# Slot numbers of all experts spread over the units of the second chunk of expert 0

## What is computed

```python
def moe_swiglu(h, w_router, w_gu_e, w_down_e):
    probs = jax.nn.softmax((hf @ w_router).astype(F32), axis=-1)
    topv, topi = lax.top_k(probs, TOP_K)                 # 2 of 8 experts
    topv = topv / jnp.sum(topv, axis=-1, keepdims=True)
    gates = jnp.sum(jax.nn.one_hot(topi, N_EXPERTS, dtype=F32) * topv[..., None], axis=1)
    for e in range(N_EXPERTS):
        out = out + gates[:, e:e + 1] * swiglu(hf, w_gu_e[e], w_down_e[e]).astype(F32)
```

## Time and profile before

| what | value |
|---|---|
| three runs | 1415.29, 1418.67, 1419.31 us |
| median | 1418.67 us |
| the profiled execution, own time | 1415.88 us |
| its span | 1414.1 us |
| mean granted TensorE clock | 0.984 of full speed |
| PE busy | 1355.0 us (96%) |
| DVE busy | 1116.7 us (79%) |
| ACT busy | 810.1 us (57%) |
| POOL busy | 242.8 us (17%) |
| DMA | 409.75 MB, mean 290 GB/s |
| chain that ended last | PE 88%, POOL 4%, DVE 3%, DMA 2% |

### The profile page before, as it was taken

How to read it: one execution, slowest core, us unless ns; L and a number is a source line. 1 busy time by engine, 2 the same in 40 slices (tenths; PEclk the granted TensorE clock), 3 DMA queues, 4 the chain that set the end, 5 groups by cost and what they waited for, 6 DMA issues and landing times.

```text
span 1414.1 us, 17000 instructions
## 1 busy us (share of the span) xinstructions
PE 1355.0 (96%) x6717; PEld 1128.6 (80%) x6717; DVE 1116.7 (79%) x1024; ACT 810.1 (57%) x808; POOL 242.8 (17%) x347
## 2 busy tenths in 40 slices
PE   4999979899999998989999999999999999999995
PEld 2787558699999986888888888888888888888884
DVE  2697766557677556658899899998998999989997
ACT  4432764523223223355687777777777777767772
POOL 4000681100000014001899300000000000000001
PEclk9999989999999999989999999999999999999998
DMA  9967445945554537537899999999999999999991
GB/s 311 366 227 248 133 144 183 333 154 178 172 169 147 190 132 248 214 135 283 267 403 390 370 412 369 375 398 347 414 373 370 412 353 388 392 355 401 373 413 51
DMA packets 119238, 409.75 MB, mean 290 GB/s; under 512 B 8385, under 2 KB 31090, under 8 KB 102258
## 3 DMA queue, kind: packets, MB, share of 16 engines
q1 hardware_dynamic: 111376, 382.24, 72.1%
q0 software_dynamic: 6704, 23.14, 5.3%
q10 hardware_dynamic: 1074, 3.23, 0.6%
HBM read 398.58 MB, written 9.99 MB: 289 GB/s over the span
## 4 chain that ended last, share of the span: by engine, by line
PE 88%; POOL 4%; DVE 3%; DMA 2%; SPq 1%; issue 1%; ACT 1%; POOLq 0%; DVEq 0%; ACTq 0%
PE ps L1763 27%; PE ps L1765 26%; PE ps L1764 26%; DMA raw<-in_ada_w 2%; PE ps L2136 1%; POOL xn L719 1%; POOL o_rstd L717 1%; SPq L501 1%; DVE ring_lo L1561 1%; PE ps L2036 1%; POOL o_msq L715 1%; PE ps L1981 1%; POOL o_eps L712 1%; PE ps L2079 1%; PE ps L2109 1%
## 5 line engine op out<-in xcount | busy, mean ns | idle before, releaser
L1561 DVE TENSOR_TENSOR ring_lo<-raw,ring_hi 128x2048 fp32r<-128x2048 f32 (+1 forms) x210 | 451.8, 2168 | 49.6 <-ACT ring_hi L1023 49.0
L1023 ACT ACTIVATE ring_hi<-raw 128x2048 fp32r<-128x2048 f32 (+1 forms) x210 | 381.2, 1819 | 124.3 <-PE ps L1765 123.2
L1763 PE MATMUL ps<-ring_hi,xe 128*128 128x512 f32 x536 | 212.2, 396 | 1.3 <-DVE xe L1612 0.8
L1765 PE MATMUL ps<-ring_lo,xe 128*128 128x512 f32 x536 | 209.9, 392 | 0.0
L1764 PE MATMUL ps<-ring_hi,xe 128*128 128x512 f32 x536 | 209.5, 391 | 0.0
L818 ACT ACTIVATE ring_hi<-raw 128x2048 fp32r<-128x2048 f32 x53 | 101.2, 1914 | 160.9 <-PE ps L1765 149.2
L1167 DVE TENSOR_TENSOR ring_lo<-raw,ring_hi 128x2048 fp32r<-128x2048 f32 x53 | 120.4, 2288 | 87.4 <-ACT ring_hi L818 87.2
L1561 DVE TENSOR_TENSOR ring_lo_more<-raw,ring_hi_more 128x2048 fp32r<-128x2048 f32 (+1 forms) x70 | 151.8, 2168 | 16.7 <-ACT ring_hi_more L1023 16.5
L1023 ACT ACTIVATE ring_hi_more<-raw 128x2048 fp32r<-128x2048 f32 (+1 forms) x70 | 127.3, 1819 | 40.1 <-PE ps L1765 39.8
L1763 PEld LDWEIGHTS ps<-ring_hi,xe 128*128 128x128 f32 x536 | 101.5, 189 | 22.1 <-DVE xe L1612 0.9
L1765 PEld LDWEIGHTS ps<-ring_lo,xe 128*128 128x128 f32 x536 | 101.2, 189 | 21.6
(11 more groups left out here) (319 smaller groups left out, 2432.4 us busy)
## 6 DMA issues: line engine op xcount, KB each, us to landing
raw<-in_w_gu_e SPq DMA_DIRECT2D x128, 1024.0 KB, 8.1
raw<-in_w_down_e SPq DMA_DIRECT2D x88, 1024.0 KB, 8.9
raw<-in_w_gu_e SPq DMA_DIRECT2D x64, 768.0 KB, 6.8
raw<-in_ada_w SPq DMA_DIRECT2D x40, 1024.0 KB, 6.0
raw<-in_w_gu SPq DMA_DIRECT2D x44, 512.0 KB, 5.0
raw<-in_w_qkv SPq DMA_DIRECT2D x12, 1024.0 KB, 10.1
raw<-in_w_down SPq DMA_DIRECT2D x11, 1024.0 KB, 5.2
raw<-in_ada_w SPq DMA_DIRECT2D x16, 512.0 KB, 12.7
```

Of the source, the lines that this page charges most:

```text
L1023: act.activation(ehi[m % RINGM][:, 0:w], raw[:, (MOE_U0 + m) % RAW, 0:w], ACT.Copy).then_inc(hi_ready, 1)
L1561: dve.tensor_tensor(elo[m % RINGM][:, 0:w], raw[:, (MOE_U0 + m) % RAW, 0:w], ehi[m % RINGM][:, 0:w].bitcast(F32), ALU.subtract).then_inc(l ...
L1763: pe.matmul(out, l_hi, r_hi, start=first, stop=False)
L1765: return pe.matmul(out, l_hi, r_lo, start=False, stop=last)
```

## The change

`number_others()` in front of unit 8 is gone. In its place `number_some(n)` runs before unit n of the second chunk of expert 0: experts 4, 5 and 6 before n = 1, experts 0, 1 and 2 before n = 3, experts 3 and 7 before n = 4, and the transposes of `selx` before n = 5. The numbers go to bank 4 and the transposes to bank 5, which the down products use first from unit 16 on. VectorE's `numbers_out` and ScalarE's copy of `selT` move from the end of the first chunk to the turn of n = 6 (unit 14). TensorE waits for both in front of unit 16 and no longer at `TURN_K`.

```diff
+NUMBERS_AT = {1: (4, 5, 6), 3: (0, 1, 2), 4: (3, 7)}
+NUMBERS_K = 5
...
                     if kind == "gu" and n == KC - 1:
                         tanh_gate(e, c)
-                        if (e, c) == (0, 0):
-                            act.wait_ge(selT_ps, 1)
-                            act.activation(selT[:], ps[:, 7, 0:TOK], ACT.Copy).then_inc(selT_sb, 1)
...
                 kind, e, c, n = MU[m]
+                if (kind, e, c, n) == ("gu", 0, 1, NUMBERS_K + 1):
+                    act.wait_ge(selT_ps, 1)
+                    act.activation(selT[:], ps[:, 5, 0:TOK], ACT.Copy).then_inc(selT_sb, 1)
...
-            numbers_of = ps[:, 6, 64:80].rearrange("p (e c) -> p e c", c=2)
+            numbers_of = ps[:, 4, 64:80].rearrange("p (e c) -> p e c", c=2)
...
                         hidden(e, c)
-                        if (e, c) == (0, 0):
-                            numbers_out()
...
                 kind, e, c, n = MU[m]
+                if (kind, e, c, n) == ("gu", 0, 1, NUMBERS_K + 1):
+                    numbers_out()
...
-            def number_others():
-                pe.wait_ge(cnt_ready, 1)
-                for e in range(N_EXP):
+            def number_some(n):
+
+                for e in NUMBERS_AT.get(n, ()):
                     number_slots(e)
-                for k in range(TILES):
-                    ins = pe.transpose(ps[:, 7, k * P:(k + 1) * P], selx[:, k, :], ident[:])
-                ins.then_inc(selT_ps, 1)
+                if n == NUMBERS_K:
+                    for k in range(TILES):
+                        ins = pe.transpose(ps[:, 5, k * P:(k + 1) * P], selx[:, k, :], ident[:])
+                    ins.then_inc(selT_ps, 1)
...
-                    if n == 0 and (e, c) == (0, 1):
-                        number_others()
+                    if (e, c) == (0, 1):
+                        number_some(n)
                     if n == 0 and NC * e + c:
                         pe.wait_ge(eh_ready, NC * e + c)
                     if n == TURN_K and (e, c) == (0, 1):
-                        pe.wait_ge(selT_sb, 1)
-                        pe.wait_ge(idx_ready, 1)
+                        pe.wait_ge(cnt_ready, 1)
...
                         if c == 0 and e:
                             pe.wait_ge(y_sb, e)
+                        elif c == 0:
+                            pe.wait_ge(selT_sb, 1)
+                            pe.wait_ge(idx_ready, 1)
```

More of the change, by code:

```diff
@@ L2116, in number_slots @@
                 for k in range(TILES):
-                    ins = pe.matmul(ps[:, 6, 64 + 2 * e:66 + 2 * e], choice[e][:, k, :], vals[:, k, e, :],
+                    ins = pe.matmul(ps[:, 4, 64 + 2 * e:66 + 2 * e], choice[e][:, k, :], vals[:, k, e, :],
                                     start=(k == 0), stop=(k == TILES - 1))
```

## The result

The changed kernel takes 1433.63 us (median of 4 runs, 1431.08 to 1436.75) against 1418.42 for the kernel before on the same chip. The ratio is 1.0125, with a 95% interval of 1.0109 to 1.0140. The forecast was 1430.8, slower, in a range of 1421 to 1441. The execution whose profile follows is the slowest of the four, 1436.75 us with a span of 1434.8.

The account below looks back on a forecast made before the run. TensorE's matmul stream was taken to bound the expert phase. 1415.88 + 3.7 (chunk 2) + 7.6 (pause) + 2.2 (clock) = 1429.4, raised to 1430.8 us, half way towards the three runs' centre; range 1421 to 1441.

Parts of the forecast that it names:

- The run fills a hole: Before unit 8, the number matmuls occupied TensorE's wait for eh_ready; without them it idles 4.78 us.
- 3.7 us more in chunk 2: Expert 0's second chunk: hole, units, records, transposes and clock total 18.0 to 18.1 us against 14.35; bounds 1.5 and 4.7.
- The clock under the spread groups: After unit 8, no second clock fall was counted under the spread records; one would add 1 to 2 us.
- `idx_ready` 28.4 us later: VectorE's numbers, taken behind unit 17's split, end at 695.0 instead of 666.66; TensorE's wait before unit 16 costs nothing.
- The pause: Expert 1's third chunk: TensorE waits 28.4 - 3.7 - 17.1 = 7.6 us for the gather of expert 2.
- The length of the chain: GpSimd's 125 small steps before the gather of expert 2 were taken to keep their length of 113.3 us.
- The second rival: GpSimd's chain gets longer, its opening 11.6 us instead of 5.3: 7.1 us on top, 1437.9 us; chance 0.20.
- Clock behind the pause: After TensorE's pause for the gather of expert 2, slow clock costs another 2.2 us.
- The first rival: GpSimd's chain is 7.6 us shorter, say all blocks at 17 us; only 3.7 us remain: 1421.0 us; chance 0.14.
- hide beside wide matmuls: Faster rival in chunk 2: spread records hide, clock never falls, chain in time; 4.1 us less, 1413.2 us; chance 0.04.
- nothing happens: Rival before unit 8: no effect, needing the wait for eh_ready over by 660.1; it ends at 664.8; no separate chance.

Follow-up runs that it names:

- e2: The changed kernel with all number matmuls and transposes in one run before unit 8 again, banks 4 and 5, read at unit 14: 1431.78 us, ratio 1.0115.
- e5: e1 with VectorE making hidden(0, 0) ahead of the split of unit 10 and the last slot matrix a turn earlier: 1418.13 us, ratio 1.0006.
- e7: e6 with hidden where the change has it, six experts numbered before unit 8 and two behind: 1415.50 us, ratio 0.9993.
- e4: The changed kernel with all numbers and transposes in one run behind unit 8, read at unit 10, GpSimd's chain in its old place: 1430.14 us, ratio 1.0100.
- e1: The changed kernel with GpSimd's chain, further_blocks(), moved behind the gather of expert 3: 1421.37 us, ratio 1.0038.
- e3: e2 with GpSimd's chain, further_blocks(), moved behind the gather of expert 3: 1415.54 us, ratio 0.9999.
- e6: e5 with five experts numbered before unit 8, three and the transposes behind it, read at unit 10: 1414.56 us, ratio 0.9984.

## Why the prediction was right, point by point

- **The run fills a hole: right.** I forecast 4.8 us of new idle time before unit 8, released by VectorE's `eh`. It was 4.61, and e2, e5 and e7 show its cause from three sides: it vanishes with the run in place, shrinks with VectorE's order, and is filled by six experts.
- **3.7 us more in chunk 2: right in kind, low by 0.7.** The marks say 4.4. One part is clock: unit 8 ran wholly at the low level, 5.3 us (667.37 to 672.65), where I had taken 4.7 us of it. (Those 4.7 were counted from 666.85; the first wide matmul of the earlier trace rows starts at 666.50, so they should have been 5.0.) The other part is a term that I did not have: the first wide matmul after a narrow group starts 0.32 us before the next one instead of 0.23, and there are four more such places, some 0.4 us.
- **The clock under the spread groups: right.** It did not fall again (0.99 from 672.5 to 693.4). In e4 the same records in one run behind the slow unit brought it down.
- **`idx_ready` 28.4 us later: right.** From the first mark it came 6.38 us later before and 35.34 us later after, a difference of 29.0. TensorE's wait in front of unit 16 cost nothing, as forecast.
- **The pause: right, but mis-sized, 12.05 us instead of 7.6.** The term was "28.4 - 3.7 - 17.1". With measured values it is 29.0 - 4.5 - 17.1 = 7.4. Three things that I had kept at their old values were each a little later: GpSimd's instruction for the gather of expert 1 took 2.42 instead of 1.03 us, and met a split of VectorE that had begun at 698.13 for 2.29 us; the chain 115.2 instead of 113.3; the gather's landing 9.2 instead of 7.8. That adds 4.7, so the form of the term was right, and what was wrong was to keep these three. e1 and e3 remove the pause by moving the chain alone.
- **The length of the chain: near, by luck, since two errors cancelled.** I had let the opening keep its 5.3 us. It took 9.7, with seven steps of 0.2 us stretched over 8.20. The Trainium skill (SBUF — State Buffer, section "Who interferes with whom") says that a VectorE instruction with two inputs in SBUF contends with a GpSimd instruction that reads SBUF, and this opening agrees. The five blocks and the closing steps took 105.5 us together instead of 108.0. The second rival, with 7.1 us on top, was right that the opening would be held up and wrong in the size: the chain grew by 1.9 us.
- **Clock behind the pause: right.** The stretch grew by 13.8 us, 12.05 of them pause, so 1.8 for 2.2 forecast.
- **The other rivals.** GpSimd was not in time. The first rival's example was also mis-sized: all blocks at 17 us would have shortened the chain by 20.4 us (3.4 + 11.5 + 5.5), not by 7.6. The records did not hide beside wide matmuls: 18 of them hold TensorE from 672.65 to 674.68 behind unit 8, the old 0.11 each. That nothing happens was excluded by the hole itself.

The forecast added 13.5 us (3.7 + 7.6 + 2.2), and the two causes give 18.2 in the profiled execution, which was the slowest of its four: 0.7 more in chunk 2, 4.4 more of pause, 0.4 less of clock. The changed runs' median is 15.2 us above the median beside it and 2.8 us above the forecast, so the forecast time came nearer than its terms did; how far the pause differs from run to run was not measured, since there is one profile of each kernel.

## What to carry to other kernels

Before moving small work off the busiest engine's queue, ask what that engine would have waited for there: here the numbers sat in a hole of 4.6 us, and outside it they cost their full price of 0.11 us a record. Then follow the semaphore that the moved work raises to every engine that waits for it, through all that is queued behind the wait; the larger loss, 12 us, came some 120 us after the numbers were ready, through the queue of GpSimd, which the edit had not touched, and where a slack of 17 us had been overdrawn. Fill a hole with what fits (e6 and e7, which are back at the kernel before or 1.8 us below it) and take a long chain that nobody needs yet out of the queue in front of a transfer that somebody needs (e1).

## What the runs showed of the hardware

- A chain of small GpSimd steps runs in step with VectorE's two-input splits. In the change its trace has 38 rows of over 1.4 us, for steps that take 0.2 to 0.3 us elsewhere, and each of them ends within 0.4 us after a split does. The chain took 113.3, 115.2, 115.2 and 120.5 us in the kernel before, the change, e2 and e4, for the same 125 steps. In the change and in e2 the opening took the same 9.68 us, in the kernel before 5.3. That the length depends on how the two engines' steps fall together is my reading; no run varied that alone.
- TensorE's low clock is not only a matter of idle time. In e4 it fell within a run of two-column matmuls in which the engine was busy throughout, after 3.7 us of it, right behind a unit of wide matmuls that had run at the low level. The same records in groups of 18 at most, with a unit in between, left it at 0.99.
- The gather of expert 2 took 9.2 us to land in the change although TensorE stood still for all of it, longer than the 7.8 of the kernel before; it took 9.7 in e2 and 9.0 in e4. The DMA engines were at 1.02 of their time in that pause (814.3 to 826.3 us). What held the gather up is not shown.
